# Mixer values computed with tokens on partitions instead of turned, bias row added by VectorE, stabiliser spread by split rows

## The chip, the cores and the metric

The kernel runs on one core of one Trainium2 chip. The metric is the device time of one execution in microseconds (us). A change of 0.2% is 4.8 us.

## What is computed

The reference runs a two-layer block over 256 latent tokens and 256 context tokens of width 1024, in float32. Each layer is a feed-forward network with a gated activation, a token mixer with three branches, and a second such network, each followed by a layer norm. What matters here is the start of the mixer, a projection of all tokens into some 9,000 columns, and two of its branches:

```python
(sb, scg, sx, mq, mk, mv, mo, mg, dq, dk, dv, gs, gm, gd) = split_cols(u @ w_in + b_in)
# mLSTM branch: 4 heads, values of 256 columns each
num = w_inter[..., None] * jnp.einsum('bhtd,bhde->bhte', qc, C) + jnp.einsum('bhts,bhse->bhte', s, vc)
h_out = num / jnp.maximum(jnp.abs(den), jnp.exp(-m_t))[..., None]
# differential attention branch: 4 heads, values of 128 columns each
w = p[:, :, 0] - lam * p[:, :, 1]
return jnp.einsum('bhqk,bhkd->bhqd', w.astype(v.dtype), v)
```

`mv` (1024 columns) and `dv` (512 columns) are the two sets of values. In both einsums the sum runs over the tokens of the values, so the engine needs them with the tokens on the 128 partitions. `m_t` is the stabiliser of the mLSTM: its running maximum must be known to every partition before the exponentials are taken.

## The kernel before

Activations are kept turned: features on the partitions, the 512 tokens along the free axis (`u_hi`, `u_lo`: the high and the low part of the mixer's input, so that three products of rounded operands give nearly float32). The weights come in **chunks** of 1024 x 128 elements. For each chunk SyncE's queue loads `raw` (2 slots), ScalarE rounds it into `w_hi` (L1362), VectorE subtracts to get `w_lo` (L1964), and TensorE multiplies 8 pieces of 128 rows three ways: 24 matmuls (L938 to L940) of 512 moving token columns into one PSUM bank, the weights being the stationary operand. ScalarE and VectorE split four chunks ahead: `ahead(base, r)`, called when chunk r comes up in either engine's program, splits chunk r+4, and waits for `chunk_used` of chunk r first, since chunk r+4 takes its slot. Only then comes the engine's own work on chunk r (the evacuation of its bank).

The order of the mixer's steps is one list per layer, `proj_order`, that every engine walks: `mq` 0 to 3; four chunks of the convolution branch; then `mk` 0 to 3 and `mv` 0 to 7 with four parts of the gate arithmetic (`gates`, on VectorE 64-row and 32-row instructions on the small tensors `gt`) between them; then `sx` 1, `sb` 1 and `cg` 2; then four heads of the mLSTM (`ml_s` scores, `ml_n` numerators, `ml_h` turns) with the chunks of other projections between their parts; then the tail with the last projections, the rotary step (`rope`, four small ScalarE copies each and three VectorE instructions) and `ysplit`; then the gate phase (`gs` 0, attention scores of the first unit, `sc` 0, ...). Chunks take PSUM banks 0 to 3 in turn (0 and 1 only beside the mLSTM).

Values before: a value chunk is computed like any other, features on partitions. ScalarE evacuates it with its bias into `scr` 4 or 5 (L1640), TensorE turns it in four transposes of 128 x 128 (`turn_v`, L1160), and VectorE copies the result to `vaug` or `dav` (L2516). There are 12 of these per layer: `mv` 0 to 7 and `dv` 0 to 3; the turn of chunk n stands one chunk later, the last two inside chunk `gs` 0. Layer 1 is the last layer: the steps named in `X_ONLY` and the gate phase then have only 256 tokens, but `mk`, `dk`, `mv` and `dv` still have 512.

Stabiliser before: VectorE writes the negated maximum of each head and direction to one row of `neg_g` (rows 0 to 3 and 64 to 67, the other rows up to 31 and 95 computed, the rest zero); at the start of each head TensorE multiplies it in float32 by a column of the identity, spread to 128 (L1188), two products into banks 4 and 5.

Of the kernel before, what the change touches and what calls it, by code (L numbers as in the profile page):

```python
# [16 lines left out]
F32 = mybir.dt.float32  # L17
# [5 lines left out]
P = 128  # L23
# [171 lines left out]


def evacuation_order(order, layer, vector):

    order = list(order)
    if vector:  # L200
        order.remove(("turn_v", 7))
        order.insert(order.index(("sx", 1)), ("turn_v", 7))
    for h in range(HEADS):
# [3 lines left out]
        elif vector:  # L207
# [7 lines left out]
EVAC_ENGINE = {"mq": "act", "mk": "dve", "mv": "act", "cg": "act", "sx": "dve", "sb": "dve",  # L215
               "mo": "act", "dv": "act", "dq": "act", "dk": "act"}
# [69 lines left out]
PROJ_BANK = [n % (2 if n in BESIDE_ML else 4) for n in range(CH_PROJ)]  # L286
SCORE_ML = (6, 7, 2, 3)
# [67 lines left out]
def build(nc, x, c, ctx, c_ctx, w_ada, b_ada, ln_g, ln_b, ffn1_up, ffn1_down, ffn2_up, ffn2_down,  # L355
# [20 lines left out]
    fold = below("fold", [P, FOLDS, P], F32)  # L376
    fold_out = nc.dram_tensor("fold_out", (P, 2 * BLOCK), F32)
# [57 lines left out]

    ysc_hi = at("ysc_hi", [P, 4, TOK], F32R, region)
# [4 lines left out]
    neg_g = at("neg_g", [P, TOK], F32, region + 32 * KB + KB // 2)  # L441
# [105 lines left out]
    def sem(name):  # L547
# [158 lines left out]
    def _(sp):  # L706
# [158 lines left out]
    def _(pe):  # L865
# [283 lines left out]
        def turn_v(layer, v):  # L1149

            kind, i = ("mv", v) if v < 8 else ("dv", v - 8)
            pe.wait_ge(evac_act, BASES[layer, "proj"][1] + PLANS[layer][kind, i][2] + 1)
            g = 12 * layer + v
            wait(pe, v_placed, g - 1)
            if v == 0:
                pe.wait_ge(gate_act, 5 * layer + 1)
            if v == 8:
                pe.wait_ge(ht_ready, HEADS * (layer + 1))
            for t in range(TT):
                m = pe.transpose(ps[value_bank(v)][:, t * P:(t + 1) * P], scr[4 + v % 2][:, t * P:(t + 1) * P], ident)  # L1160
            m.then_inc(v_turned, 1)
# [65 lines left out]
        def scores(layer, v):  # L1227
# [6 lines left out]
            if v == 0:  # L1234
                pe.wait_ge(v_placed, 12 * (layer + 1))
# [34 lines left out]
        def gated_chunk(layer, step):  # L1270
# [7 lines left out]
            if step == ("ml", 0):  # L1278
# [3 lines left out]
                  ready=(yda_ready, 4 * layer + 1) if step == ("da", 0) else None,  # L1282
                  after_k=3 if step == ("gs", 0) else None, then=lambda: (turn_v(layer, 10), turn_v(layer, 11)))

        def mixer(layer):
            t = slice(t0_of(layer), TOK)
            for step in ORDERS[layer]:
                if step[0] in EVAC_ENGINE:
# [7 lines left out]
                elif step[0] == "turn_v":  # L1296
                    turn_v(layer, step[1])
# [46 lines left out]
    def _(act):  # L1344
# [255 lines left out]
        def proj(layer, step):  # L1600
# [5 lines left out]
            if kind in ("sx", "mk"):  # L1606
                return
# [18 lines left out]
            elif kind in ("mv", "dv"):  # L1626
                v = i if kind == "mv" else 8 + i
                wait(act, v_turned, 12 * layer + v - 1)
                if v in (8, 9):
                    act.wait_ge(yf_ready, y_number(layer, "sb", 3) + 1)  # L1630
                dst, func = scr[4 + v % 2][:, t0:TOK], ACT.Identity
# [120 lines left out]
        def gated_chunk(layer, step):  # L1752
# [4 lines left out]
            if kind in SIGMOIDS:  # L1757
# [9 lines left out]
                elif k == 2:  # L1767
                    act.wait_ge(v_turned, 12 * (layer + 1))
# [172 lines left out]
    def _(dve):  # L1941
# [566 lines left out]
        def turn_v(layer, v):  # L2508
            g = 12 * layer + v
            dve.wait_ge(v_turned, g + 1)  # L2510
            src = ps[value_bank(v)][:, :].rearrange("p (t n) -> p t n", t=TT)
            if v < 8:
                dst = vaug[:, :, v // 2, (v % 2) * P:(v % 2 + 1) * P]
            else:
                dst = dav[:, :, v - 8, :]
            dve.tensor_copy(dst, src).then_inc(v_placed, 1)  # L2516
# [18 lines left out]
        def gates(layer, part):  # L2535
            raw_g, lf, ln1, ia, la = gt[1], gt[2], gt[3], gt[4], gt[5]
            ones, fsum, gmax, top = gt[6], gt[7], gt[2], gt[0]
            if part == 0:

                dve.memset(vaug[:, :, :, 256:257], 1.0)  # L2540
                dve.memset(neg_g[32:64, :], 0.0)
                dve.memset(neg_g[96:128, :], 0.0)
# [12 lines left out]
            elif part == 2:  # L2555
                link(dve.memset(ones[0:64, :], 1.0))
# [3 lines left out]
            else:  # L2560
# [149 lines left out]
        def mixer(layer):  # L2710
            t0 = t0_of(layer)
            for step in evacuation_order(ORDERS[layer], layer, vector=True):
                if step[0] == "mq" and layer == DEPTH - 1:
                    continue
                if step[0] in EVAC_ENGINE:
# [7 lines left out]
                elif step[0] in ("turn_v", "rope"):  # L2723
                    {"turn_v": turn_v, "rope": rope}[step[0]](layer, step[1])
            for step in [("turn_v", 10), ("turn_v", 11)] + GATE_ORDERS[layer]:
# [11 lines left out]
                elif step[0] == "turn_v":  # L2737
                    turn_v(layer, step[1])
# [152 lines left out]
```

## Time and profile before

| | |
|---|---|
| median of 3 runs | 2405.98 us (2404.79 to 2406.38) |
| profiled execution, own time | 2403.49 us |
| its span, first to last instruction | 2401.5 us |
| TensorE matmul busy | 2362.2 us, 98% of the span |
| VectorE busy | 1586.5 us, 66% |
| ScalarE busy | 1003.3 us, 42% |
| GpSimd busy | 175.9 us, 7% |
| mean granted TensorE clock | 0.998 |

The share of TensorE is near 100% because matmuls overlap each other in the pipeline, so it says that the engine seldom stands still, not that it works at its peak. The mixer's projections stand at 372 to 752 us (layer 0, from the second network's end on) and 1790 to 2034 us (layer 1).

### The profile page before, as it was taken

How to read it: one execution, taken by the hardware profiler on the slowest of the kernel's cores; microseconds unless marked ns; L12 is line 12 of the kernel's file. 1: busy time of each engine (PE TensorE's matmuls, PEld its weight loads, DVE VectorE, ACT ScalarE, POOL GpSimd, SP SyncE). 2: the span in 40 equal slices, each digit the busy share in tenths (PEclk: the TensorE clock that was granted, in tenths of full speed). 3: DMA queues.
4: the chain of work that ended last, by engine and by line, in shares of the span. 5: the costliest groups of instructions: out<-in, count | busy, mean ns of one | idle time of the engine just before them, and what ended most of it. 6: DMA issues, size and time to landing. Idle time of an engine off the chain costs nothing.

```text
span 2401.5 us, 35644 instructions
## 1 busy us (share of the span) xinstructions
PE 2362.2 (98%) x13050; PEld 2034.4 (85%) x13050; DVE 1586.5 (66%) x2616; ACT 1003.3 (42%) x1666; POOL 175.9 (7%) x168
## 2 busy tenths in 40 slices
PE   7999999999999999999999999999999999999998
PEld 4888888887888778898888898888898898998998
DVE  6898577445546555568885368886666556667875
ACT  6432224434335334363222254322255456555554
POOL 0111010000000000021111000111100000001220
PEclk9999999999999999999999999999999999999999
DMA  8687464232222322327773327775534333556654
GB/s 277 214 253 246 122 211 132 80 93 74 62 65 77 97 79 62 114 76 238 247 242 118 97 79 242 240 236 178 167 95 126 107 102 101 163 146 180 192 158 133
DMA packets 557847, 355.31 MB, mean 148 GB/s; under 512 B 15078, under 2 KB 515344, under 8 KB 557712
## 3 DMA queue, kind: packets, MB, share of 16 engines
q1 hardware_dynamic: 556264, 353.13, 49.4%
q8 instruction: 85, 1.39, 0.2%
q10 hardware_dynamic: 1448, 0.38, 0.1%
q14 instruction: 50, 0.41, 0.1%
HBM read 335.63 MB, written 17.83 MB: 147 GB/s over the span
## 4 chain that ended last, share of the span: by engine, by line
PE 90%; DVE 3%; ACT 3%; issue 2%; DMA 2%; SPq 1%; POOL 0%; DVEq 0%; ACTq 0%; POOLq 0%
PE ps L938 26%; PE ps L940 26%; PE ps L939 26%; PE ps L1223 2%; PE ps L1021 1%; PE ps L1022 1%; PE ps L1023 1%; PE ps L1238 1%; PE ps L1199 1%; PE ps L1255 1%; DMA raw<-in_ffn_up 1%; SPq L718 1%; DVE w_lo L1964 1%; ACT w_hi L1362 1%; PE ps L1169 0%
## 5 line engine op out<-in xcount | busy, mean ns | idle before, releaser
L938 PE MATMUL ps<-u_hi,w_hi 128*128 128x512 f32 (+2 forms) x2368 | 859.5, 363 | 1.3 <-DVE scr L2282 1.1
L940 PE MATMUL ps<-u_hi,w_lo 128*128 128x512 f32 (+2 forms) x2368 | 848.4, 358 | 0.0
L939 PE MATMUL ps<-u_lo,w_hi 128*128 128x512 f32 (+2 forms) x2368 | 847.9, 358 | 0.0
L1964 DVE TENSOR_TENSOR w_lo<-raw,w_hi 128x1024 fp32r<-128x1024 f32 (+3 forms) x432 | 497.6, 1153 | 513.5 <-ACT w_hi L1362 511.4
L1362 ACT ACTIVATE w_hi<-raw 128x1024 fp32r<-128x1024 f32 (+3 forms) x432 | 425.4, 985 | 915.4 <-PE ps L940 818.4
L938 PEld LDWEIGHTS ps<-u_hi,w_hi 128*128 128x128 f32 x2368 | 447.3, 189 | 66.2 <-DVE scr L2282 1.3
L940 PEld LDWEIGHTS ps<-u_hi,w_lo 128*128 128x128 f32 x2368 | 447.1, 189 | 65.9
L939 PEld LDWEIGHTS ps<-u_lo,w_hi 128*128 128x128 f32 x2368 | 447.5, 189 | 62.7
L2345 DVE SCALAR_TENSOR_TENSOR ada_acc<-ada_in_up,cs,ada_acc 128x512 f32<-128x512 f32 x378 | 273.2, 786 | 0.2 <-DMA ada_in_up<-in_w_ada 0.2
L938 PE MATMUL ps<-g_hi,w_hi 128*128 128x512 f32 (+1 forms) x704 | 244.3, 347 | 1.3 <-DVE scr L2302 1.3
L940 PE MATMUL ps<-g_hi,w_lo 128*128 128x512 f32 (+1 forms) x704 | 241.5, 343 | 0.0
L939 PE MATMUL ps<-g_lo,w_hi 128*128 128x512 f32 (+1 forms) x704 | 241.4, 343 | 0.0
L1913 POOL TENSOR_TENSOR fold<-fold 128x512 f32<-128x512 f32 x64 | 85.1, 1329 | 947.4 <-DMA fold<-fold_out 944.9
L938 PEld LDWEIGHTS ps<-g_hi,w_hi 128*128 128x128 f32 x704 | 133.5, 190 | 18.1 <-issue 1.5
L939 PEld LDWEIGHTS ps<-g_lo,w_hi 128*128 128x128 f32 x704 | 133.5, 190 | 16.2 <-issue 0.7
L940 PEld LDWEIGHTS ps<-g_hi,w_lo 128*128 128x128 f32 x704 | 133.4, 190 | 15.6
L1523 ACT ACTIVATE g_hi<-scr 128x512 f32 (+1 forms) x66 | 41.8, 633 | 187.4 <-DVE scr L2261 182.8
L1021 PE MATMUL ps<-u_hi,w_hi 128*128 128x256 f32 (+1 forms) x320 | 93.9, 293 | 9.3 <-DVE u_lo L2091 6.6
L1964 DVE TENSOR_TENSOR w_lo<-h,w_hi 128x1024 fp32r<-128x1024 f32 (+2 forms) x66 | 72.3, 1096 | 31.1 <-ACT w_hi L1362 30.9
L1022 PE MATMUL ps<-u_lo,w_hi 128*128 128x256 f32 (+1 forms) x320 | 91.7, 286 | 0.0
L1023 PE MATMUL ps<-u_hi,w_lo 128*128 128x256 f32 (+1 forms) x320 | 91.6, 286 | 0.0
L1903 POOL TENSOR_TENSOR scr<-h 128x256 f32<-128x256 f32 x3 | 5.5, 1827 | 1008.7 <-DVE h L2149 1008.7
(299 smaller groups left out, 2974.8 us busy)
## 6 DMA issues: line engine op xcount, KB each, us to landing
raw<-in_ffn_up SPq DMA_DIRECT2D x152, 512.0 KB, 4.0
raw<-in_w_in SPq DMA_DIRECT2D x132, 512.0 KB, 3.6
ada_in_up<-in_w_ada SPq DMA_DIRECT2D x108, 512.0 KB, 4.3
raw<-in_ffn_down SPq DMA_DIRECT2D x67, 384.0 KB, 3.5
fold_out<-ada_acc SPq DMA_DIRECT2D x32, 512.0 KB, 3.0
fold<-fold_out SPq DMA_DIRECT2D x32, 512.0 KB, 5.3
raw<-in_ffn_down SPq DMA_DIRECT2D x42, 320.0 KB, 3.3
h<-in_ffn_up SPq DMA_DIRECT2D x22, 512.0 KB, 3.8
```

What stands on the lines that cost most here:

```text
L938: pe.matmul(ps[bank][:, cols_of], wh, a_hi, start=a, stop=False)
L939: pe.matmul(ps[bank][:, cols_of], wh, a_lo, start=False, stop=False)
L940: m = pe.matmul(ps[bank][:, cols_of], wl, a_hi, start=False, stop=b)
L1021: pe.matmul(ps[q][:, own], wh, u_hi[:, k, own], start=(k == 0), stop=False)
L1022: pe.matmul(ps[q][:, own], wh, u_lo[:, k, own], start=False, stop=False)
L1023: m = pe.matmul(ps[q][:, own], wl, u_hi[:, k, own], start=False, stop=(k == KD - 1))
L1223: m = pe.matmul(ps[NUMERATOR[t % 2][n]][:, 0:257], pw[:, n, s, t * P:(t + 1) * P], vaug[:, s, head, :], start=(s == keys[0]), stop=(s == k ...
L1362: act.activation(hi, whole, ACT.Copy).then_inc(hi_done, 1)
L1523: act.activation(g_hi[:, 2 * i + q // 2, t0:TOK], scr[2 + q // 2][:, t0:TOK], ACT.Copy).then_inc(g_hi_done, 1)
L1913: pool.tensor_tensor(fold[:, 0:n, :], fold[:, 0:n, :], fold[:, n:2 * n, :], ALU.add).then_inc(fold_half, 1)
L1964: dve.tensor_tensor(lo, whole, hi.bitcast(F32), ALU.subtract).then_inc(lo_done, 1)
L2345: dve.scalar_tensor_tensor(ada_acc[:, s, :], w, by, ada_acc[:, s, :], ALU.mult, ALU.add).then_inc(ada_mul, 1)
```

## The change

The 12 value chunks of a layer become 3 groups of 4 (`mv` 0-3, `mv` 4-7, `dv` 0-3). A chunk now holds 2 of the 8 row pieces by 512 columns instead of 8 pieces by 128 columns: the same 512 KB, the same two splits. TensorE takes 128 tokens of `u_hi` or `u_lo` as the stationary operand and lets 512 weight columns move; it goes through the 4 token tiles, each with its own PSUM bank 0 to 3, and a bank is complete only with the group's fourth chunk. VectorE then adds the bias, which lies on all partitions as a row (`value_bias`, loaded once per layer by two broadcasting transfers), and writes to `vaug` or `dav`. The turns, ScalarE's evacuations of values and the copies behind the turns are gone. `mo` 6 and the `dv` chunks change places, so that the four `dv` chunks stand together at the end. The stabiliser's rows are written as a high and a low row part in the format of the fast products, and the spreading product is done in that format with a column that adds both.

```diff
@@ proj_order
-        if n >= 5:
-            order.append(("turn_v", n - 5))
...
-    order += [("rope", 0), ("rope", 4), ("mo", 6), ("rope", 1), ("rope", 5), ("ysplit", 0), ("ysplit", 1)]
-    order += [("mo", 7), ("rope", 2), ("rope", 6), ("ysplit", 2), ("ysplit", 3)]
-    order += [("dv", 1), ("turn_v", 8), ("rope", 3), ("rope", 7), ("ysplit", 4), ("ysplit", 5)]
-    order += [("dv", 2), ("turn_v", 9), ("ysplit", 6), ("ysplit", 7), ("dv", 3)]
+    order += [("rope", 0), ("rope", 4), ("mo", 7), ("rope", 1), ("rope", 5), ("ysplit", 0), ("ysplit", 1)]
+    order += [("dv", 0), ("rope", 2), ("rope", 6), ("ysplit", 2), ("ysplit", 3)]
+    order += [("dv", 1), ("rope", 3), ("rope", 7), ("ysplit", 4), ("ysplit", 5)]
+    order += [("dv", 2), ("ysplit", 6), ("ysplit", 7), ("dv", 3)]
@@ SyncE, mixer
+                if step[0] in VALUES:
+                    slot, _, split_before = raw_place(base + PLANS[layer][step][0], 0)
+                    k, col = step[1] % 4 * 2, in_col(SEC[step[0]] + step[1] // 4 * 4)
+                    sp.wait_ge(lo_done, split_before)
+                    sp.dma_start(raw[:, slot, :].rearrange("p (k n) -> p k n", k=2), src[:, k:k + 2, col:col + BLOCK]
+                                 ).then_inc(raw_in[slot], 16)
...
+                if step == ("mq", 3):
+                    if layer:
+                        sp.wait_ge(*proj_done(layer - 1, CH_PROJ - 1))
+                    for kind, n in (("mv", 2), ("dv", 1)):
+                        first, col = VALUES[kind] * BLOCK, in_col(SEC[kind])
+                        sp.dma_start(value_bias[:, first:first + n * BLOCK],
+                                     b_in[layer, col:col + n * BLOCK].partition_broadcast(P)).then_inc(bias_landed, 16)
@@ TensorE
+        def values(layer, step):
+
+            kind, i = step
+            r, n, _, _ = PLANS[layer][step]
+            base, part = BASES[layer, "proj"][0], i % 4
+            slot = (base + r) % SPLIT
+            pe.wait_ge(lo_done, base + r + 1)
+            if part == 0 and kind == "dv":
+                pe.wait_ge(hsum_ready, nth_out(layer, HEADS - 1, TT - 1) + 1)
             for t in range(TT):
+                own = slice(t * P, (t + 1) * P)
+                if part == 0:
+                    earlier = [m for m in range(n) if PROJ_BANK[m] == t]
+                    pe.wait_ge(*proj_done(layer, earlier[-1]))
+                for e in range(2):
+                    k, cols_of = 2 * part + e, slice(e * BLOCK, (e + 1) * BLOCK)
+                    wh, wl = w_hi[:, slot, cols_of], w_lo[:, slot, cols_of]
+                    pe.matmul(ps[t][:, :], u_hi[:, k, own], wh, start=(k == 0), stop=False)
+                    pe.matmul(ps[t][:, :], u_lo[:, k, own], wh, start=False, stop=False)
+                    m = pe.matmul(ps[t][:, :], u_hi[:, k, own], wl, start=False, stop=(k == KD - 1))
+                if part == 3 and t < TT - 1:
+                    m.then_inc(v_summed, 1)
+            m.then_inc(chunk_used, 1)
...
-                    m = pe.matmul(ps[4 + n][:, t0:TOK], ident[own, row:row + 1].to_broadcast([64, P]),
+                    m = pe.matmul(ps[4 + n][:, t0:TOK], head_rows[own, head:head + 1].to_broadcast([64, P]),
                                   neg_g[own, t0:TOK], start=True, stop=True)
@@ VectorE
+        def values(layer, step):
+
+            kind, i = step
+            base = BASES[layer, "proj"][0]
+            r = PLANS[layer][step][0]
+            ahead(base, r)
+            if i % 4 < 3:
+                return
+            group = VALUES[kind] + i // 4
+            bias = value_bias[:, group * BLOCK:(group + 1) * BLOCK]
+            dve.wait_ge(bias_landed, 32 * (layer + 1))
+            for t in range(TT):
+                if t < TT - 1:
+                    dve.wait_ge(v_summed, 3 * (3 * layer + group) + t + 1)
+                else:
+                    dve.wait_ge(chunk_used, base + r + 1)
...
+                dve.tensor_tensor(dst, ps[t][:, :].rearrange("p (h n) -> p h n", h=n),
+                                  bias.rearrange("p (h n) -> p h n", h=n), ALU.add).then_inc(evac_dve, 1)
@@ VectorE, gates part 3
-                flip(top[96:128, :], fsum[32:64, :])
+                flip(top[96:128, :], fsum[32:64, :]).then_inc(gate_dve, 1)
+
+                turned = ones[64:96, :]
                 dve.tensor_copy(neg_g[0:32, :], gmax[0:32, :])
-                flip(neg_g[64:96, :], gmax[32:64, :]).then_inc(gate_dve, 1)
+                link(flip(turned, gmax[32:64, :]))
+                link(dve.tensor_copy(neg_g[64:96, :], turned))
+                dve.tensor_tensor(neg_g[32:64, :], gmax[0:32, :], neg_g[0:32, :].bitcast(F32), ALU.subtract)
+                dve.tensor_tensor(neg_g[96:128, :], turned, neg_g[64:96, :].bitcast(F32), ALU.subtract
+                                  ).then_inc(ng_split, 1)
```

The order of instructions moves at three places on which the prediction rests. The first is VectorE in layer 0 from the end of the gate arithmetic (its part 3) on. Before, the split of a chunk (`w_lo`) and the copy of the previous value chunk from bank 6 or 7 take turns:

```order
L2568 COPY neg_g_104<-gt2_119 32x512
L2529 COPY neg_g_104<-gt2_119 32x256
L2530 COPY neg_g_104<-gt2_119 32x256
L1964 TENSOR_TENSOR w_lo_56<-raw_54,w_hi_55 128x1024 [waits chunk_used,hi_done]
L2516 COPY vaug_103<-ps6 128x4x128 [waits v_turned]
L1964 TENSOR_TENSOR w_lo_56<-raw_54,w_hi_55 128x1024 [waits chunk_used,hi_done]
L2516 COPY vaug_103<-ps7 128x4x128 [waits v_turned]
```

The same place in the changed kernel (numbers behind the tensors' names and of the lines differ between the two):

```order
L2595 CAST neg_g_106<-gt2_121 32x512
L2552 COPY gt6_125<-gt2_121 32x256
L2553 COPY gt6_125<-gt2_121 32x256
L2597 CAST neg_g_106<-gt6_125 32x512 [waits dve_chain]
L2598 TENSOR_TENSOR neg_g_106<-gt2_121,neg_g_106 32x512 [waits dve_chain]
L2599 TENSOR_TENSOR neg_g_106<-gt6_125,neg_g_106 32x512
L1974 TENSOR_TENSOR w_lo_57<-raw_55,w_hi_56 128x1024 [waits chunk_used,hi_done]
L2538 TENSOR_TENSOR vaug_105<-ps0,value_bias_51 128x2x256 [waits v_summed,bias_landed]
L2538 TENSOR_TENSOR vaug_105<-ps1,value_bias_51 128x2x256 [waits v_summed]
L2538 TENSOR_TENSOR vaug_105<-ps2,value_bias_51 128x2x256 [waits v_summed]
L2538 TENSOR_TENSOR vaug_105<-ps3,value_bias_51 128x2x256 [waits chunk_used]
```

What moved: three instructions more at the end of part 3, and the four bank evacuations of the first group all stand behind the split that belongs to `mv` 3, which itself waits for `chunk_used`.

The second place is TensorE in layer 0 where `mv` 3 ends and `mv` 4 begins. Before, with the turn of a value chunk (the transposes of `scr`) between two chunks:

```order
L938 MATMUL ps0<-u_hi_52,w_hi_55 128x512
L939 MATMUL ps0<-u_lo_53,w_hi_55 128x512
L940 MATMUL ps0<-u_hi_52,w_lo_56 128x512
L1160 MATMUL ps7<-con_57,scr5_81 128x128 [waits v_placed,evac_act]
L1160 MATMUL ps7<-con_57,scr5_81 128x128 x3
L938 MATMUL ps1<-u_hi_52,w_hi_55 128x512 [waits lo_done,evac_act]
```

And now:

```order
L1175 MATMUL ps3<-w_hi_56,u_hi_53 128x512
L1176 MATMUL ps3<-w_hi_56,u_lo_54 128x512
L1177 MATMUL ps3<-w_lo_57,u_hi_53 128x512
L1175 MATMUL ps0<-w_hi_56,u_hi_53 128x512 [waits evac_dve,lo_done]
L1176 MATMUL ps0<-w_hi_56,u_lo_54 128x512
L1177 MATMUL ps0<-w_lo_57,u_hi_53 128x512
```

What moved: no transposes stand between the chunks, the weights are the moving operand (named first), and the chunk's first matmul waits for VectorE's evacuation of bank 0, which the chunk just ended has filled.

The third place is VectorE at the end of layer 0's tail, from the last `ysplit` to the first maximum of the attention. Before:

```order
L2462 TENSOR_TENSOR yml_lo_102<-ht_125,yml_hi_101 128x512 [waits y_hi_done] x2
L1964 TENSOR_TENSOR w_lo_56<-raw_54,w_hi_55 128x1024 [waits chunk_used,hi_done]
L2516 COPY dav_113<-ps4 128x4x128 [waits v_turned]
L2516 COPY dav_113<-ps5 128x4x128 [waits v_turned]
L1964 TENSOR_TENSOR w_lo_56<-raw_54,w_hi_55 128x1024 [waits chunk_used,hi_done]
L2617 TENSOR_REDUCE att_73<-ps4 128x1 [waits sc_ready]
```

And now:

```order
L2472 TENSOR_TENSOR yml_lo_104<-ht_127,yml_hi_103 128x512 [waits y_hi_done] x2
L1974 TENSOR_TENSOR w_lo_57<-raw_55,w_hi_56 128x1024 [waits chunk_used,hi_done]
L2538 TENSOR_TENSOR dav_115<-ps0,value_bias_51 128x512 [waits v_summed,bias_landed]
L2538 TENSOR_TENSOR dav_115<-ps1,value_bias_51 128x512 [waits v_summed]
L2538 TENSOR_TENSOR dav_115<-ps2,value_bias_51 128x512 [waits v_summed]
L2538 TENSOR_TENSOR dav_115<-ps3,value_bias_51 128x512 [waits chunk_used]
L1974 TENSOR_TENSOR w_lo_57<-raw_55,w_hi_56 128x1024 [waits chunk_used,hi_done]
L2648 TENSOR_REDUCE att_74<-ps4 128x1 [waits sc_ready]
```

What moved: the copies of banks 4 and 5 are gone, and banks 0 to 3 are evacuated between the splits of the last `dv` chunk and of `gs` 0, whose matmuls need bank 0.

## Rows read from the trace of the kernel before

**Rows 1.** The page: busy time of TensorE; windows, busy time of each engine, layer 0's value chunks

```profile
PE 2362.2 (98%) x13050; PEld 2034.4 (85%) x13050; DVE 1586.5 (66%) x2616; ACT 1003.3 (42%) x1666; POOL 175.9 (7%) x168
...
488.00:542.00 54.00, 54.00 (x255) 44.72 (x254) 25.72 (x39) 18.08 (x23) 0.00 (x0) 1.00 0.33 95
```

**Rows 2.** Timeline of TensorE, layer 0: start us, duration us, instruction

```profile
494.48 0.39 PE L938 MATMUL ps<-u_hi,w_hi 128*128 128x512 f32 x1
...
499.69 0.39 PE L940 MATMUL ps<-u_hi,w_lo 128*128 128x512 f32 x1
499.93 0.60 PE L1160 MATMUL ps<-con,scr 128*128 128x128 f32 x4
...
505.86 0.60 PE L1160 MATMUL ps<-con,scr 128*128 128x128 f32 x4
```

**Rows 3.** The chain that ended last, in order of time: the spreading products, both layers

```profile
553.40 1.06 PE ps L1188 x4
...
1896.54 0.63 PE ps L1188 x4
```

**Rows 4.** Timeline of TensorE, end of layer 1's tail

```profile
2022.22 0.66 PE L1160 MATMUL ps<-con,scr 128*128 128x128 f32 x4 [1.76 <-ACT scr L1640]
...
2031.89 0.28 PE L940 MATMUL ps<-u_hi,w_lo 128*128 128x256 f32 x1
2032.42 1.13 PE L1238 MATMUL ps<-dqk 64*128 64x512 f32 x4 [0.25 <-DVE dav L2516]
```

**Rows 5.** Timeline of ScalarE, layer 0, behind the chunk that ends in rows 2

```profile
500.12 1.06 ACT L1362 ACTIVATE w_hi<-raw 128x1024 fp32r<-128x1024 f32 x1 [3.81 <-PE ps L940]
```

**Rows 6.** Timeline of VectorE, layer 0: a split, a copy, gates part 3, the next split

```profile
507.14 1.23 DVE L1964 TENSOR_TENSOR w_lo<-raw,w_hi 128x1024 fp32r<-128x1024 f32 x1 [4.05 <-ACT w_hi L1362]
508.29 0.68 DVE L2516 COPY vaug<-ps 128x512 f32<-128x512 f32 x1
508.89 0.67 DVE L2561 TENSOR_TENSOR gt<-gt,gt 64x512 f32<-64x512 f32 x1
...
513.06 1.23 DVE L1964 TENSOR_TENSOR w_lo<-raw,w_hi 128x1024 fp32r<-128x1024 f32 x1 [0.23 <-ACT w_hi L1362]
```

**Rows 7.** Timelines of VectorE and ScalarE: bank 3 of `mk` 3 evacuated, the split behind `mv` 0

```profile
493.94 0.75 DVE L2477 TENSOR_SCALAR kt<-ps,cols 128x512 f32<-128x512 f32 x1
...
1844.48 0.74 DVE L2477 TENSOR_SCALAR kt<-ps,cols 128x512 f32<-128x512 f32 x1
...
494.68 1.06 ACT L1362 ACTIVATE w_hi<-raw 128x1024 fp32r<-128x1024 f32 x1 [2.03 <-PE ps L940]
...
1845.65 1.06 ACT L1362 ACTIVATE w_hi<-raw 128x1024 fp32r<-128x1024 f32 x1 [2.88 <-PE ps L940]
```

**Rows 8.** Timelines: splits of a chunk of half size; the rotary copies of ScalarE in layer 1's tail

```profile
754.60 0.62 ACT L1362 ACTIVATE w_hi<-raw 128x512 fp32r<-128x512 f32 x1
...
2022.19 3.42 ACT L1706 ACTIVATE scr<-dqk 32x256 f32<-32x256 f32 x8
...
2038.40 0.69 DVE L1964 TENSOR_TENSOR w_lo<-raw,w_hi 128x512 fp32r<-128x512 f32 x1
```

**Rows 9.** Windows, entry to layer 1's mixer (DMA share and GB/s last); issues: KB, us to landing

```profile
1790.00:1800.00 10.00, 10.00 (x85) 9.95 (x84) 6.52 (x12) 4.76 (x10) 0.00 (x0) 1.00 0.00 0
...
gain_row<-in_ln_g SPq DMA_DIRECT2D x1, 512.0 KB, 4.0
```

**Rows 10.** Windows: us, busy (x instructions) of PE, PEld, DVE, ACT, POOL, granted clock; TensorE's longest pause

```profile
36.00:42.00 6.00, 2.13 (x13) 1.34 (x11) 3.17 (x7) 3.84 (x7) 0.00 (x0) 1.00 1.17 295
...
43.00:49.00 6.00, 5.25 (x24) 4.96 (x24) 3.83 (x4) 6.00 (x12) 0.00 (x0) 0.51 0.56 151
...
50.00:52.00 2.00, 2.00 (x19) 2.00 (x18) 1.71 (x5) 2.00 (x5) 0.00 (x0) 1.00 0.71 274
...
2020.50:2022.20 1.70, 0.00 (x0) 0.00 (x0) 1.67 (x5) 1.68 (x4) 0.00 (x0) 1.00 0.00 0
...
41.65 0.35 PE L1021 MATMUL ps<-u_hi,w_hi 128*128 128x256 f32 x1 [3.10 <-DVE u_lo L2091]
```

More of the change, by code:

```diff
@@ L286 @@
 PROJ_BANK = [n % (2 if n in BESIDE_ML else 4) for n in range(CH_PROJ)]
+assert all(n % 4 == v[1] % 4 for n, v in NTH_PROJ.items() if v[0] in VALUES)
 SCORE_ML = (6, 7, 2, 3)
@@ L1183, in ml_scores @@
             if s == 0:
-                pe.wait_ge(v_placed, 12 * layer + 8)
+                pe.wait_ge(evac_dve, BASES[layer, "proj"][2] + PLANS[layer]["mv", 7][3] + 1)
+                pe.wait_ge(ng_split, layer + 1)
                 wait(pe, ht_ready, u)
                 for n in range(2):
-                    own, row = slice(64 * n, 64 * n + 64), 64 * n + head
-                    m = pe.matmul(ps[4 + n][:, t0:TOK], ident[own, row:row + 1].to_broadcast([64, P]),
+                    own = slice(64 * n, 64 * n + 64)
+                    m = pe.matmul(ps[4 + n][:, t0:TOK], head_rows[own, head:head + 1].to_broadcast([64, P]),
                                   neg_g[own, t0:TOK], start=True, stop=True)
@@ L1281, in gated_chunk @@
             chunk(base + n, (base + n) % SPLIT, n % 4, of(hi, lo, range(GATE_KN[kind]), t), t,
-                  ready=(yda_ready, 4 * layer + 1) if step == ("da", 0) else None,
-                  after_k=3 if step == ("gs", 0) else None, then=lambda: (turn_v(layer, 10), turn_v(layer, 11)))
+                  ready=(yda_ready, 4 * layer + 1) if step == ("da", 0) else None)
         def mixer(layer):
@@ L1287, in mixer @@
             for step in ORDERS[layer]:
-                if step[0] in EVAC_ENGINE:
+                if step[0] in VALUES:
+                    values(layer, step)
+                elif step[0] in EVAC_ENGINE:
                     proj(layer, step)
@@ L1605, in proj @@
             ahead(base, r)
[L1606 removed]
+            if kind in ("sx", "mk", "mv", "dv"):
                 return
@@ L1625, in proj @@
                 dst, func = qt[:, i, t0:TOK], ACT.Identity
[L1626 to L1631, printed above, removed]
             elif kind == "mo":
@@ L2506, in proj @@
                                          ALU.add, ALU.mult).then_inc(yf_ready, 1)
[L2508 to L2516, printed above, removed]
+        def values(layer, step):
[13 more added lines that the diff above has]
+                    dve.wait_ge(chunk_used, base + r + 1)
+                if kind == "mv":
+                    dst, n = vaug[:, t, 2 * group:2 * group + 2, 0:2 * P], 2
+                else:
+                    dst, n = dav[:, t, :, :], HEADS
+                dve.tensor_tensor(dst, ps[t][:, :].rearrange("p (h n) -> p h n", h=n),
+                                  bias.rearrange("p (h n) -> p h n", h=n), ALU.add).then_inc(evac_dve, 1)
         def rope(layer, i):
@@ L2555, in gates @@
             elif part == 2:
+                if layer == 0:
+                    link(dve.tensor_reduce(fsum[:, 0:HEADS], ident.rearrange("p (g n) -> p n g", g=4)[:, 0:HEADS, :],
+                                           AXX, ALU.add))
+                    link(dve.tensor_copy(head_rows[:, :], fsum[:, 0:HEADS]))
                 link(dve.memset(ones[0:64, :], 1.0))
@@ L2714, in mixer @@
                     continue
-                if step[0] in EVAC_ENGINE:
+                if step[0] in VALUES:
+                    values(layer, step)
+                elif step[0] in EVAC_ENGINE:
                     proj(layer, step)
@@ L2722, in mixer @@
                     (ml_scores if step[0] == "ml_s" else ml_numerator)(layer, *step[1:])
-                elif step[0] in ("turn_v", "rope"):
-                    {"turn_v": turn_v, "rope": rope}[step[0]](layer, step[1])
-            for step in [("turn_v", 10), ("turn_v", 11)] + GATE_ORDERS[layer]:
+                elif step[0] == "rope":
+                    rope(layer, step[1])
+            for step in GATE_ORDERS[layer]:
                 if step[0] in GATE_KN:
```

43 lines of the change are left out of this document (11 added, 32 removed), and 2 rows, old and new, of the table fill.

## The prediction

> **What bounds the kernel now.** I read the page first: TensorE's matmuls are busy 98% of the span, VectorE 66%, ScalarE 42% [rows 1]. Then the windows over the stretch that the change rewrites: in the 54 us of layer 0's value chunks TensorE is busy for all 54.00, while VectorE has 26 and ScalarE 18 [rows 1]. So whatever TensorE is spared there counts in full, and whatever it has to wait for counts in full too; VectorE's and ScalarE's busy time is worth nothing by itself. The timeline of TensorE gives the unit of account: a chunk of 24 matmuls starts at 494.48, its last one at 499.69, the next instruction at 499.93 [rows 2], so a chunk is 5.44 us and a 512-column matmul 0.227. Only in layer 1's tail does TensorE stand still: 1.76 us before one turn, where ScalarE's evacuation is late, and some 0.4 us before the first attention scores (last matmul at 2031.89, 0.12 long as a step, scores at 2032.42), where VectorE's copies are late [rows 4].
>
> **The change part by part: what TensorE is spared.**
> Turns: from one turn to the next, with a chunk between, is 505.86 - 499.93 = 5.93 us [rows 2]; less 5.44 leaves 0.49 for a turn. 24 turns: 11.8 us.
> Spreading: two products take 1.06 us in layer 0 and 0.63 in layer 1 [rows 3]. In the fast format I price them like any other matmul of as many columns: 2 x 0.23 and 2 x 0.12, which saves 0.60 and 0.39 a head, over 4 heads each 4.0 us. Below, the saving could be 0, above, not more than the 6.8 that they take.
> The two waits of layer 1's tail go with the evacuations and copies that caused them: 2.2 us.
> ScalarE's 24 evacuations of values and VectorE's copies cost TensorE nothing but that, so they are worth nothing more. Together 18.0 us.
> The matmuls of the values themselves stay 24 a chunk with 512 moving columns and 128 x 128 weights loaded for each. The trace has no matmul with `u_hi` stationary, but all its 512-column steps are alike, so I take 0.227 again.
>
> **What TensorE now waits for.** This is where I had to look behind the diff. Before, a chunk's bank was needed again four chunks later. Now a group fills all four banks, and they become complete in its last chunk, so the next chunk's first matmul needs bank 0 at once. VectorE can't deliver it at once: `values` calls `ahead` first, which waits for `chunk_used` of the chunk just ended, and for ScalarE's split behind it. The early signals after each token tile (`v_summed`) are therefore of no use; the evacuations start only behind both splits. One such wait, in rows:
> - ScalarE begins 0.20 us after the next matmul could have started (499.69 + 0.23 against 500.12), and its split takes 1.06 [rows 2, 5];
> - VectorE's split holds its engine for 1.15 (507.14 to 508.29) [rows 6];
> - the evacuation of one bank: 0.68 as the copy from PSUM [rows 6], 0.75 as the add and multiply [rows 7]; I take 0.69;
> - signals between three engines and filling TensorE again: I take 0.25, an estimate from the 0.20 above.
> That is 3.35 us, and it falls on `mv` 4 (behind the first group) and on `sx` 1 (behind the second), in both layers. Behind `dv` 3 the split is that of a half-size chunk, 0.62 and 0.69 less the overlap of 0.08 [rows 8]: 2.4 us before `gs` 0, in both layers. The remaining three banks come every 0.65 us while TensorE needs 1.36 us for a tile, so they cost nothing.
>
> Two of these are worse. At `mv` 4 VectorE is late for another reason: part 3 of the gates follows the split of `mv` 2 and ran from 508.89 to 512.83 (513.06 less 0.23 idle), 3.94 us [rows 6], and has one copy and two subtractions of 32 rows more, near 0.46 + 2 x 0.61 = 1.7 by the 0.67 of the 64-row instruction [rows 6]. From the start of `mv` 2's split this ends after 1.15 + 3.94 + 1.7 = 6.8 us, but the split of `mv` 3 could start after 5.44. Before, 1.35 us of lateness there hurt nobody, since splits run four chunks ahead; now bank 0 stands behind it. The wait at `mv` 4 becomes 4.7 us. And the first group needs bank 3 in its first chunk, at its last tile, which `mk` 3 filled only one chunk ago. In layer 0 `mv` 0 ended at 494.48 (494.68 less 0.20), its last tile began 1.36 earlier, at 493.12; the evacuation of bank 3 ended at 494.69 [rows 7]. With 0.25 that is 1.8 us; in layer 1, by the same rows (1845.45, 1844.09, 1845.22), 1.4. Behind TensorE's waiting matmul stands all else of the mixer, so nothing hides it.
>
> Sum of waits: 3.2 (bank 3) + 2 x 4.7 + 2 x 3.35 + 2 x 2.4 = 24.1 us.
>
> **Costed at nothing.** The two broadcasts of the bias (512 and 256 KB) go into SyncE's queue behind `mq` 3's load. The like of the first took 4.0 us to land [rows 9], so both hold the queue for some 6 us, ahead of the loads of `cg` 0 and `sx` 0. What hides them is 10 us in which no transfer runs before those weights are split in layer 1 [rows 9]; without that cover, up to 6 us. In the tail the `dv` chunks no longer need a ScalarE evacuation, and ScalarE's pace there, per chunk a split of 1.06 [rows 5], eight rotary copies of 3.42 together [rows 8] and two splits of the mLSTM's output, each half a split's size, is 5.5 us in layer 0 against 5.44 of a chunk: it just keeps up, and `gs` 0 doesn't wait longer for it.
>
> **The clock.** In this trace TensorE paused once for 3.10 us, and in the 6 us around that pause it was busy for only 2.13; directly after it the granted clock was 0.51, the 1.2 GHz level, for the window of 6 us, and 1.00 again later [rows 10]. A 256-column matmul then took 5.25 / 24 = 0.22 us instead of 2.00 / 19 = 0.105 [rows 10], so such a stretch costs up to 3 us. The shorter pause of 1.76 us in layer 1 left the clock at 1.00 [rows 10]. Two pauses of 4.7 us and two of 3.35 are new. I take two falls, one for each long pause, at 2 us each, between nothing and 3, since part of the slow stretch lies in the pause itself: +4 us; four falls at 3 us would be +12. The Trainium skill, "TensorE: Matmul & The Clock Gate", section Part 1, says that "the default state is throttled, and activity releases the throttle". By that rule each long pause is paid a second time; the trace agrees with it once.
>
> **Sum.** -18.0 + 24.1 = +6.1 us; with the clock +10.1. Against the profiled execution (span 2401.5, 2403.49 with what lies around it) that gives 2413.6; the median of the runs shown is 2.49 us higher, so I forecast 2416 for it.
>
> **Rivals.**
> *No fall of the clock.* The pauses come as worked out, but TensorE's short wait leaves the clock alone, as at 1.76 us. Then +6.1: 2412, with 2409 to 2415 by the bounds of 0.25 us on each wait and the spreading. For it: only one fall is in the trace, after a pause that had little work before it. Against: 4.7 us is longer than any pause inside a layer before.
> *The value matmuls run at another step.* This is the one that ends faster: 576 matmuls (24 x 12 x 2) change operands. If a step with the weights moving were shorter by more than 10.9 / 576 = 0.019 us (0.208 instead of 0.227), the kernel would be faster by over 0.2% without a fall; at 0.030 shorter it would be 2395. For it: nothing but that the trace has no such matmul. Against: the steps of all 512-column matmuls are alike.
> *The bias transfers are not hidden.* Then the loads of `cg` 0 and `sx` 0 land late in layer 1, up to 6 us more: 2420 to 2422. For it: of the 10 us only some 4 are left if they run at the pace of the 4.0 us. Against: those 4.
> *The waits are absorbed.* If half of the 24.1 us were given back (VectorE and ScalarE finding their work done when the mLSTM begins), the result would be no change, 2404 to 2408. Against: TensorE has no waits in layer 0 that could shrink [rows 1].
>
> **Chances.** Waits with a fall of the clock 0.52 (2413 to 2423, my number 2416); no fall 0.28; transfers 0.08; absorbed 0.07; faster step 0.05. The range that leaves out 2 in 10 is 2409 to 2422. What a measurement can tell from no change is 0.2%, 4.8 us: faster than 2401.2 only by the step, 0.05; up to 2410.8 are the absorbed case and the lower part of the one without a fall, 0.16; slower 0.79.
>
> **What would show it.** In the profile after: no transposes of `scr`, chunks of 5.44 us one behind the other, and TensorE waiting for VectorE's evacuation of `vaug` twice and of `dav` once a layer, 4.7, 3.35 and 2.4 us, and for `kt` once, 1.4 to 1.8. The page's row of granted clock should fall in two slices. I am wrong if TensorE's waits in the two mixers sum to under 18 us, if the value matmuls' step isn't 0.227, or if the spreading products keep their time.

## The result, and the profile after

The changed kernel takes 2423.09 us (median of 4 runs, 2418.61 to 2423.79), the kernel before 2406.18 on the same chip (4 runs, 2404.79 to 2407.22): 0.7% slower, ratio 1.007 with a 95% interval of 1.0057 to 1.0082. That is 7.1 us above the predicted 2416 and 1.1 above the range. The direction was right, the size was not.

The profiled execution is the quickest of the four: 2418.61 us, span 2416.6, mean granted clock 0.995; the others had 0.992, 0.992 and 0.991. The page's row of TensorE, and the windows over layer 0's value chunks, which answer to [rows 1]:

```profile
PE 2354.4 (97%) x12938; PEld 2026.2 (84%) x12938; DVE 1591.8 (66%) x2620; ACT 990.1 (41%) x1642; POOL 174.8 (7%) x168
```

```profile
488.00:542.00 54.00, 47.88 (x199) 38.78 (x198) 24.73 (x40) 13.21 (x14) 0.00 (x0) 0.94 0.30 81
```

TensorE has 112 instructions less and is busy 7.8 us less, yet the end is later: in the 54 us that it filled before, it now works for 47.88. The waits of TensorE (engine, line, what it waited for: us in total, times, longest) name what it stood for:

```profile
PE ps L1175 <- DVE vaug L2538: 9.3, 2, 4.7
...
PE ps L947 <- DVE dav L2538: 6.0, 2, 3.0
PE ps L947 <- DVE vaug L2538: 6.0, 2, 3.0
...
PE ps L1175 <- DVE kt L2487: 2.5, 2, 1.5
```

None of the four stood in the trace of before, and the two waits of layer 1's tail [rows 4] are gone. Each wait is at the forecast place. The longest one, at `mv` 4 in layer 0, on TensorE's timeline (start us, duration us, instruction; in brackets the idle time before it):

```profile
513.30 0.39 PE L1176 MATMUL ps<-w_hi,u_lo 128*128 128x512 f32 x1
513.53 0.39 PE L1177 MATMUL ps<-w_lo,u_hi 128*128 128x512 f32 x1
518.58 0.77 PE L1175 MATMUL ps<-w_hi,u_hi 128*128 128x512 f32 x1 [4.67 <-DVE vaug L2538]
519.14 0.63 PE L1176 MATMUL ps<-w_hi,u_lo 128*128 128x512 f32 x1
519.57 0.63 PE L1177 MATMUL ps<-w_lo,u_hi 128*128 128x512 f32 x1
```

and the same moment on VectorE's:

```profile
509.61 1.23 DVE L1974 TENSOR_TENSOR w_lo<-raw,w_hi 128x1024 fp32r<-128x1024 f32 x1 [4.16 <-ACT w_hi L1380]
510.75 0.68 DVE L2586 TENSOR_TENSOR gt<-gt,gt 64x512 f32<-64x512 f32 x1
...
515.89 0.68 DVE L2599 TENSOR_TENSOR neg_g<-gt,neg_g 32x512 fp32r<-32x512 f32 x1
516.61 1.23 DVE L1974 TENSOR_TENSOR w_lo<-raw,w_hi 128x1024 fp32r<-128x1024 f32 x1
517.75 2.48 DVE L2538 TENSOR_TENSOR vaug<-ps,value_bias 128x512 f32<-128x512 f32 x4
```

The steps before the pause are 0.227 us apart, so the value matmuls cost what all others cost. The group's last matmul starts at 513.53, and all four banks are complete soon after. But VectorE is in part 3 of the gates until 516.6, then does the split of the next chunk (1.14 until its next instruction), and only at 517.75 begins the first evacuation; TensorE goes on 0.83 us later. Behind the pause the steps are 0.43 apart: the clock has fallen. The windows of this execution behind the six pauses for `vaug` and `dav` (us, busy time of PE, PEld, DVE, ACT, POOL, granted clock, DMA share, GB/s):

```profile
519.00:525.00 6.00, 6.00 (x17) 4.64 (x17) 1.23 (x3) 0.00 (x0) 0.00 (x0) 0.59 0.31 85
546.10:550.00 3.90, 3.88 (x17) 3.23 (x18) 1.76 (x3) 0.00 (x0) 0.00 (x0) 1.00 0.49 134
753.70:758.00 4.30, 4.29 (x19) 3.56 (x20) 1.74 (x3) 0.00 (x0) 0.00 (x0) 1.00 0.21 61
1876.70:1883.00 6.30, 6.26 (x16) 4.95 (x17) 1.69 (x3) 0.00 (x0) 0.00 (x0) 0.55 0.32 86
1904.40:1908.00 3.60, 3.59 (x30) 3.59 (x31) 1.75 (x3) 0.41 (x1) 0.00 (x0) 1.00 0.61 146
2044.40:2049.00 4.60, 4.59 (x31) 3.70 (x32) 2.08 (x4) 1.41 (x2) 0.00 (x0) 1.00 0.19 57
```

In the mixers it has two falls, behind the two long pauses, as forecast. One more, before the first network (granted clock 0.50 from 43 to 49 us), stands in the trace of before as well [rows 10] and isn't of the change. The spreading products, by TensorE's timeline of layer 0 and layer 1, take 0.44 and 0.31 us for two (to the start of the scores), where [rows 3] had 1.06 and 0.63:

```profile
563.16 0.50 PE L1207 MATMUL ps<-neg_g,head_rows 64*128 64x512 f32 x2
563.60 1.98 PE L1218 MATMUL ps<-qt,kt 128*128 128x512 f32 x4
...
1913.67 0.39 PE L1207 MATMUL ps<-neg_g,head_rows 64*128 64x256 f32 x2
1913.98 0.70 PE L1218 MATMUL ps<-qt,kt 128*128 128x256 f32 x2
```

### The profile page after: what moved, and what is told of

It reads as the page before. It is cut to its first block, busy times and chain, and to the rows that moved or that the text cites. A ratio compares the mean times of both kernels' runs of the same rounds, so it can differ in the third digit from the quotient of the medians.

```text
span 2416.6 us, 35344 instructions
## 1 busy us (share of the span) xinstructions
PE 2354.4 (97%) x12938; PEld 2026.2 (84%) x12938; DVE 1591.8 (66%) x2620; ACT 990.1 (41%) x1642; POOL 174.8 (7%) x168
## 4 chain that ended last, share of the span: by engine, by line
PE 89%; DVE 4%; ACT 3%; issue 2%; DMA 1%; SPq 1%; POOL 0%; DVEq 0%; ACTq 0%; POOLq 0%
PE ps L947 25%; PE ps L949 24%; PE ps L948 24%; PE ps L1242 2%; PE ps L1175 2%; PE ps L1177 2%; PE ps L1176 2%; PE ps L1030 1%; PE ps L1031 1%; PE ps L1032 1%; ACT w_hi L1380 1%; PE ps L1257 1%; DVE w_lo L1974 1%; PE ps L1218 1%; PE ps L1274 1%
## 5 line engine op out<-in xcount | busy, mean ns | idle before, releaser
L947 PE MATMUL ps<-u_hi,w_hi 128*128 128x512 f32 (+2 forms) x2176 | 782.4, 360 | 13.4 <-DVE dav L2538 6.0
L949 PE MATMUL ps<-u_hi,w_lo 128*128 128x512 f32 (+2 forms) x2176 | 772.6, 355 | 0.0
L948 PE MATMUL ps<-u_lo,w_hi 128*128 128x512 f32 (+2 forms) x2176 | 772.3, 355 | 0.0
L947 PEld LDWEIGHTS ps<-u_hi,w_hi 128*128 128x128 f32 x2176 | 410.8, 189 | 73.6 <-DVE vaug L2538 6.9
L949 PEld LDWEIGHTS ps<-u_hi,w_lo 128*128 128x128 f32 x2176 | 410.7, 189 | 58.2
L948 PEld LDWEIGHTS ps<-u_lo,w_hi 128*128 128x128 f32 x2176 | 411.0, 189 | 55.7
L2355 DVE SCALAR_TENSOR_TENSOR ada_acc<-ada_in_up,cs,ada_acc 128x512 f32<-128x512 f32 x378 | 279.8, 801 | 0.0
L1175 PE MATMUL ps<-w_hi,u_hi 128*128 128x512 f32 x192 | 77.4, 403 | 11.8 <-DVE vaug L2538 9.3
```

What stands on the lines that cost most here:

```text
L947: pe.matmul(ps[bank][:, cols_of], wh, a_hi, start=a, stop=False)
L948: pe.matmul(ps[bank][:, cols_of], wh, a_lo, start=False, stop=False)
L949: m = pe.matmul(ps[bank][:, cols_of], wl, a_hi, start=False, stop=b)
L1175: pe.matmul(ps[t][:, :], u_hi[:, k, own], wh, start=(k == 0), stop=False)
L2355: dve.scalar_tensor_tensor(ada_acc[:, s, :], w, by, ada_acc[:, s, :], ALU.mult, ALU.add).then_inc(ada_mul, 1)
```

## The experiments

The theory was: the change spares TensorE what was forecast and loses it to waits for banks, at which the clock falls as well. The rivals: something in the new form costs time by itself (the step, the bias row, the wider tile), or the gain was never there.

**The changed kernel again** (`e0_again`, no edit), because one quick execution had given the picture of the clock.

> The changed kernel once more, for the spread of its clock. If each execution has at least the two falls at mv 4 and further ones at the pauses of 3.2 us in most, its times lie in steps of about 2.5 us from 2416 to 2425, in line with the granted clock (0.0014 lower for a fall). If the clock is not what separates the executions, time and clock are not related.

It took 2423.23 us (2422.96 to 2425.4, 5 runs), ratio 1.0077 (1.0063 to 1.009). Its waits are the same to 0.1 us, but the clock was low behind each of the six pauses. The windows at the same six places:

```profile
519.00:523.00 4.00, 3.85 (x10) 3.12 (x11) 1.80 (x4) 0.00 (x0) 0.00 (x0) 0.57 0.47 131
546.00:550.00 4.00, 4.00 (x12) 3.10 (x12) 1.49 (x3) 0.00 (x0) 0.00 (x0) 0.57 0.48 131
755.00:759.00 4.00, 4.00 (x11) 3.20 (x12) 1.71 (x3) 0.00 (x0) 0.00 (x0) 0.62 0.22 66
1879.50:1884.00 4.50, 4.44 (x11) 3.50 (x12) 1.71 (x3) 0.00 (x0) 0.00 (x0) 0.50 0.42 117
1907.00:1911.00 4.00, 4.00 (x24) 4.00 (x25) 1.61 (x3) 0.00 (x0) 0.00 (x0) 0.67 0.47 131
2048.30:2053.00 4.70, 4.70 (x26) 4.57 (x28) 1.70 (x3) 0.07 (x1) 0.00 (x0) 0.64 0.19 56
```

One pause of equal length shows it best. TensorE's timeline at `sx` 1 of layer 0 in this execution:

```profile
545.75 0.50 PE L947 MATMUL ps<-u_hi,w_hi 128*128 128x512 f32 x1 [3.01 <-DVE vaug L2538]
546.09 0.39 PE L948 MATMUL ps<-u_lo,w_hi 128*128 128x512 f32 x1
...
546.65 0.63 PE L947 MATMUL ps<-u_hi,w_hi 128*128 128x512 f32 x1
547.08 0.63 PE L948 MATMUL ps<-u_lo,w_hi 128*128 128x512 f32 x1
```

and in the profiled execution of the result:

```profile
546.12 0.50 PE L947 MATMUL ps<-u_hi,w_hi 128*128 128x512 f32 x1 [3.01 <-DVE vaug L2538]
546.46 0.39 PE L948 MATMUL ps<-u_lo,w_hi 128*128 128x512 f32 x1
...
546.92 0.40 PE L947 MATMUL ps<-u_hi,w_hi 128*128 128x512 f32 x1
547.15 0.39 PE L948 MATMUL ps<-u_lo,w_hi 128*128 128x512 f32 x1
```

Same pause of 3.01 us, same instructions; once the steps are 0.43 us, once 0.23. From such steps the price of a fall can be read. Behind the long pauses of the result's execution, 12 steps took 5.26 us and 13 steps 5.67, where at the full clock, with the 0.11 us longer first step of a restart at that clock, they take 2.83 and 3.06: 2.4 and 2.6 us. In this execution the same reckoning gives 1.5, 1.6 and 1.4 us in layer 0 and 2.3 at layer 1's `mv` 4. The last two are in 256-column steps: from the first matmul behind the pause to the 41st it takes 6.39 and 7.52 us here, 4.90 and 6.03 in the result's execution, so 1.5 us each. Together that is 9.8 us.

**Evacuate first** (`e1_evac_first`). In VectorE's `values` the four evacuations come before the split ahead:

```diff
             r = PLANS[layer][step][0]
-            ahead(base, r)
             if i % 4 < 3:
+                ahead(base, r)
                 return
...
                 dve.tensor_tensor(dst, ps[t][:, :].rearrange("p (h n) -> p h n", h=n),
                                   bias.rearrange("p (h n) -> p h n", h=n), ALU.add).then_inc(evac_dve, 1)
+            ahead(base, r)
```

> The changed kernel, with VectorE's four evacuations of a value group ahead of the split in the same step instead of behind it. If the waits for banks are the cause (18.0 us spared, the rest is waits and the clock), the pauses at sx 1 and gs 0 vanish, the one at mv 4 shrinks from 4.8 to about 3.6 us (gates part 3 still stands in front), those for mk 3's bank stay at 1.6 and 1.2: about 7 us faster than before without a fall of the clock, about 2 us faster with two falls: 2399 to 2404 us. If something else in the change costs time (the new matmul form, the wider loads, the bias transfers), it stays above 2410 us.

Measured 2402.32 us (2399.21 to 2407.81, 10 runs), ratio 0.9989 (0.998 to 0.9998): the slowdown is gone. The waits in its profile:

```profile
PE ps L1175 <- DVE vaug L2538: 7.1, 2, 3.5
...
PE ps L1175 <- DVE kt L2487: 2.5, 2, 1.5
```

The pauses at `sx` 1 and layer 0's `gs` 0 have vanished, and of layer 1's `gs` 0 a wait of 0.7 us is left: with the split out of the way, VectorE follows the token tiles while TensorE still computes. At `mv` 4 a wait of 3.5 us remains, since part 3 of the gates still stands ahead of the evacuations. In the profiled run (2403.64, clock 0.995) the steps behind both of these pauses of 3.53 us are 0.43. The ten times follow the clock: 2399.2 us at 0.997 and 0.996, 2407.81 at 0.994, so here too the same pauses seem to bring more or fewer falls.

**Part 3 of the gates later, splits still first** (`e5_gates3_only`):

```diff
     order = list(order)
+    if vector:
+        order.remove(("gates", 3))
+        order.insert(order.index(("mv", 3)) + 1, ("gates", 3))
```

> The changed kernel with only VectorE's part 3 of the gates moved behind mv 3; the splits still stand ahead of the evacuations. The pause at mv 4 falls from 4.8 to 3.2 us, so all six bank pauses of the groups are 3.2 us long. Waits 3.2 us less than in the changed kernel. If pauses of 3.2 us don't bring the clock down, the two falls go as well (5 us): granted clock 0.997 in every run and some 2410 to 2411 us. If they do in some executions, the clock lies at 0.991 to 0.996 and the runs spread over 2411 to 2420 us.

Measured 2417.43 us (2416.3 to 2421.38, 5 runs), ratio 1.0053 (1.0039 to 1.0067), clock 0.991 to 0.994. The waits:

```profile
PE ps L1178 <- DVE vaug L2541: 6.2, 2, 3.1
...
PE ps L950 <- DVE vaug L2541: 6.0, 2, 3.0
PE ps L950 <- DVE dav L2541: 6.0, 2, 3.0
PE ps L1178 <- DVE kt L2490: 2.5, 2, 1.5
```

So `mv` 4's pause is now like the others, 3.1 us: the gates were 1.6 us of it, the two splits and one evacuation the rest. No pause is long any more, and still steps of 0.43 us follow three of the six in this profile: both at `mv` 4 (3.10 us) and layer 0's `gs` 0 (3.00), while 3.01 at `sx` 1 left the clock alone.

**Both edits** (`e2_evac_gates3`).

> As e1, with VectorE's part 3 of the gates moved behind mv 3's evacuations. By the theory of the waits the pause at mv 4 goes too, only those for mk 3's bank are left (2.9 us together), no pause is long enough for the clock to fall: about 15 us faster than before, 2390 to 2393 us, granted clock 0.998 in each run. If the falls of the clock have another cause than the long pauses, the clock stays near 0.992.

Measured 2391.78 us (2391.41 to 2392.82, 4 runs), ratio 0.9945 (0.993 to 0.996), the clock 0.997 in every run. Of the four waits only `kt`'s 2.5 us is left, and 0.7 for `dav` in layer 1. Each kernel set against the kernel before on its own chip, one edit gave 19.5 us, the other 5.0, both together 30.1. The rest comes from `mv` 4, where either edit alone leaves a pause of 3.1 or 3.5 us with its fall of the clock, and both together leave nothing.

**Part 1 of the gates behind `mk` 3 as well** (`e3_evac_gates31`), two more lines of the same kind:

```diff
+        order.remove(("gates", 1))
+        order.insert(order.index(("mk", 3)) + 1, ("gates", 1))
```

> As e2, with VectorE's part 1 of the gates moved behind mk 3, so that bank 3 is free earlier. The theory of the waits gives 2.5 us more than e2, about 17.5 us faster than before: 2387 to 2390 us. A rival that the ScalarE split, held up by its own part 1 of the gates, is late too leaves it within 1 us of e2.

Measured 2389.25 us (2388.98 to 2390.35, 5 runs), ratio 0.9935 (0.9922 to 0.9949). The windows over the value chunks and VectorE's timeline at the same place as above:

```profile
488.00:542.00 54.00, 54.00 (x239) 44.45 (x238) 30.35 (x48) 14.99 (x16) 0.00 (x0) 1.00 0.36 98
```

```profile
508.88 1.28 DVE L2543 TENSOR_TENSOR vaug<-ps,value_bias 128x512 f32<-128x512 f32 x2
510.72 0.69 DVE L2543 TENSOR_TENSOR vaug<-ps,value_bias 128x512 f32<-128x512 f32 x1 [0.56 <-PE ps L1182]
512.08 0.69 DVE L2543 TENSOR_TENSOR vaug<-ps,value_bias 128x512 f32<-128x512 f32 x1 [0.67 <-PE ps L1182]
513.17 1.23 DVE L1979 TENSOR_TENSOR w_lo<-raw,w_hi 128x1024 fp32r<-128x1024 f32 x1 [0.40 <-ACT w_hi L1385]
514.32 0.68 DVE L2592 TENSOR_TENSOR gt<-gt,gt 64x512 f32<-64x512 f32 x1
```

TensorE is busy all 54.00 us again. VectorE now waits for TensorE between evacuations, the order the change was built for; the split comes after, and the gates last. VectorE does more in this stretch than in any other kernel here (30.35 us), and it costs nothing.

**The best version once more** (`e8_best_again`).

> The best version once more, unchanged, to see whether its time holds: 2388 to 2391 us, ratio 0.9925 to 0.9945, granted clock 0.996 to 0.997 in each run. If pauses near 1 us also brought the clock down in some executions, some runs would lie 2 us or more above that at a clock of 0.995 or less.

Measured 2388.13 us (2387.27 to 2388.39, 5 runs) against 2404.7, ratio 0.9931 (0.9917 to 0.9945), clock 0.997 in each. It holds, and it beats the kernel before by 16.6 us.

**The best version without the stabiliser's part** (`e7_values_only`): the float32 product with a column of the identity, the old part 3 and the two memsets are back.

> The best version so far (evacuations first, gate parts 3 and 1 behind their evacuations), with the stabiliser's part of the change undone: the float32 spreading product, the old third gate part and the memsets are back, the values stay with tokens on partitions. Theory (the values' part carries the gain once its waits are gone; the spreading adds what its rows show, 3.8 us, of which the run of that part alone gave about 2 over the whole kernel): 2391.5 to 2393.5 us, 12 to 14 us faster than before, ratio 0.994 to 0.995, TensorE's granted clock near 0.997. Rival (the two parts help each other, the gain comes mostly of the spreading): less than 8 us faster, over 2397 us.

Measured 2392.92 us (2391.0 to 2394.22, 5 runs), ratio 0.9949 (0.9936 to 0.9963). The values' part carries about 12 of the 16.6 us.

**The stabiliser's part alone** (`e4_spread_only`), on the kernel before. The heart of it:

```diff
-                    own, row = slice(64 * n, 64 * n + 64), 64 * n + head
-                    m = pe.matmul(ps[4 + n][:, t0:TOK], ident[own, row:row + 1].to_broadcast([64, P]),
+                    own = slice(64 * n, 64 * n + 64)
+                    m = pe.matmul(ps[4 + n][:, t0:TOK], head_rows[own, head:head + 1].to_broadcast([64, P]),
```

> The kernel before with the stabiliser's part of the change alone (split rows, fast spreading product). The two products of a head fall from 1.06 to 0.44 us in layer 0 and from 0.63 to 0.3 in layer 1, and nothing waits for the longer part 3 of the gates: 3.8 us faster than before, 2402.4 us. If the extra VectorE work showed up in TensorE's way, it would be no faster.

Measured 2402.99 us (2401.5 to 2405.08, 11 runs) against 2404.94, ratio 0.999 (0.9981 to 0.9999): 2 us where the rows give 3.8, which the interval still takes in. Between `e7_values_only` and `e8_best_again` the same part was worth 4.8. The profiled executions settle it. From the first matmul with the gates' weights (`wg_hi`) to the reciprocal of `ssq` at the end of the attention, the two mixers take 475.2 and 310.4 us here against 477.6 and 311.6 before, 3.6 us less together; between `e7_values_only` and `e8_best_again` it is 3.4. The profile of this kernel also has a pause of 1.88 us ahead of layer 1's mixer, in a part that no edit touches, and the clock low behind it (0.52), which hides part of the gain:

```profile
1765.90 0.51 PE L940 MATMUL ps<-g_hi,u_hi 128*128 128x256 f32 x1 [1.88 <-DVE u_lo L1967]
```

```profile
1765.90:1769.30 3.40, 3.40 (x16) 3.40 (x17) 2.82 (x5) 1.15 (x2) 0.00 (x0) 0.52 0.57 157
```

**A half-size split behind `dv` 1 and `dv` 3** (`e6_half_split`). The two chunks that are split there, `sc` 0 and `sc` 1, have only 4 pieces; the changed kernel splits the space of 8, and TensorE reads only the 4, so the edit leaves out nothing that is used:

```diff
-            ahead(base, r)
+            ahead(base, r, kn=4 if step in (("dv", 1), ("dv", 3)) else KD)
```

> The changed kernel with the weights of sc 0 and sc 1 split at their half size behind dv 1 and dv 3, as the forecast had priced it. The pause before gs 0 becomes 2.4 instead of 3.2 us in both layers, all else stays. If the pause has another origin than the two splits, it stays 3.2.

One run, 2419.69 us, clock 0.993. The wait for `dav`, 6.0, 2, 3.0 before, in its profile:

```profile
PE ps L947 <- DVE dav L2538: 4.1, 2, 2.0
```

and layer 0's pause on TensorE's timeline:

```profile
754.12 0.71 PE L947 MATMUL ps<-u_hi,w_hi 128*128 128x512 f32 x1 [2.05 <-DVE dav L2538]
```

Halving ScalarE's and VectorE's split behind `dv` 3 takes 1.0 us off this pause, in both layers, and off no other, so the splits in front are a part of it that was forecast too small. Though layer 0's pause is only 2.05 us long, the steps behind it are 0.43. The total of one run says nothing beyond that.

## Why the prediction was off, step by step

- **Spared, -18.0 us: borne out.** The best version, which keeps all of the change and has hardly a wait left (the longest that is new, for `dav`, is 1.0 us), gains 16.6 us. Measured as above from `wg_hi` to `ssq`, its two mixers are 15.8 us shorter than before; with that wait some 17 us are spared, so about 1 us of the 18.0 isn't found. The step of 0.227 and the hidden bias transfers (TensorE waits for no weights at layer 1's entry) held too. The rivals of a faster step and of late transfers are out.
- **Waits, +24.1 us: places right, 1.9 us short.** From start to start, less a step, the pauses are 1.6 and 1.2 us (`mv` 0; forecast 1.8 and 1.4), 4.8 twice (4.7), 3.2 twice (3.35) at `sx` 1 and 3.2 twice at `gs` 0, and each restart's first step is 0.11 longer. Sum: 2.8 + 9.6 + 12.6 + 0.9 = 26.0 with rounding. The error is `gs` 0, forecast at 2.4 with "the split is that of a half-size chunk". It isn't: `ahead` in `proj` and `values` splits whole pieces, and [rows 8] shows the half-size ones behind the chunks after it. With half-size splits, in `e6_half_split`, the pause is indeed near the price: 2.2 us by the same reckoning. So the full-size split of `sc` 1 behind `dv` 3 costs 1 us a layer, and nothing needs it.
- **The clock, +4 us: the step that failed.** "I take two falls, one for each long pause, at 2 us each." The size of a fall was right (1.4 to 2.6 us in these two executions), and in the profiled one so was the number. But in `e0_again` pauses of 3.0 us brought a fall too, six in all and 9.8 us (the prediction had not counted the two at `gs` 0, which it put at 2.4 us), and the medians of both sets are alike, as are the clocks (0.991 to 0.993). I had taken the 3.35 us pauses to behave like the one of 1.76 that left the clock alone, though the only fall in the trace of before stood behind a pause of 3.10, shorter than these [rows 10]. The row nearest in length spoke for a fall at each. My bound was "four falls at 3 us would be +12"; with it the forecast would have been 2424.
- **The sum again, with the measured terms.** -18.0 + 26.0 = +8.0. With 5.0 for two falls, 13.0: in the profiled execution the two mixers are 13.8 us longer than before. With 9.8 for six, 17.8: in `e0_again` they are 18.3 longer. The rest of the whole difference lies ahead of the first mixer, where nothing was changed: 1.2 us in the profiled execution, 1.8 in `e0_again`, of which some 0.5 are made up later. The first low stretch of the clock ends at 49 us in the one and at 51 in the other.
- **Absorbed waits: out.** Nothing of the 26 us was given back later. Every pause in the mixer shifts the end by its length.

What I had as the cause is thereby shown and not only argued: order on VectorE alone, with the same instructions, moves the kernel from 17 us slower to 16 us faster than before. That `e0_again`'s picture of six falls is that of most executions is an inference from the clocks and times alone; only two were profiled. What stays open is why equal pauses bring the clock down in one execution and not in the next.

## What to carry to other kernels

When an accumulation fills every bank, its evacuation is the next thing that the matmul engine waits for. An early signal for each bank is worth nothing if the engine that should use it stands, in its own order, at something else; so put evacuations first, prefetch work and long small-tile arithmetic behind them. When a change that should win loses, look for the pause behind it before giving the change up: here three moved calls were worth some 33 us. And where a pause of a matmul engine is about as long as one behind which a trace shows a fall of the clock, put the price of the fall into the range for each such pause, not only for the longest.

## What was unexpected in the hardware

The same kernel with the same pause (3.01 us before the same instruction) got a granted clock of 1.00 behind it in one execution and 0.57 in another. In the eleven profiles, pauses of 1.0 to 1.8 us never brought a fall, but one of 1.88 us did (in `e4_spread_only`), of two of 2.05 us one did, those of 3.0 to 3.1 us in the mixers in some cases, those of 3.5 and 4.7 us each time. Before the first network, where TensorE is little busy around the pause too (2.13 of 6 us in [rows 10]), a pause of 2.55 us (3.10 in the kernel before) had a low clock soon behind it in all eleven. A fall in the mixers cost 1.4 to 2.9 us, the most in `e5_gates3_only` at `gs` 0. So the time of a kernel with such pauses isn't that of one profile: `e1_evac_first` ran between 2399.2 and 2407.8 us, the best version between 2387.3 and 2390.4 in its ten runs. The clock is not all of such a spread: the kernel before ran between 2403.6 and 2409.0 in 21 runs at 0.996 to 0.998.
